# A wait for the end of each 256-token sum of squares on TensorE, in a four-layer model on one core

## The reference

```python
def rms_norm(x, g):
    xf = x.astype(jnp.float32)
    y = xf * lax.rsqrt(jnp.mean(xf * xf, axis=-1, keepdims=True) + RMS_EPS)
    return (y * g.astype(jnp.float32)).astype(x.dtype)

h = h + swiglu(rms_norm(h, norm_ffn[layer]), ffn_w_gu[layer], ffn_w_down[layer])
```

## Time and profile before

| | |
|---|---|
| three runs | 3108.95, 3109.23, 3134.92 us |
| median | 3109.23 us |
| profiled execution: span from first to last instruction | 3133.1 us |
| the profiled execution's own time (the only one of the three that holds its span) | 3134.92 us |
| TensorE products, and the time they are busy | 25968, 3121.2 us (100%) |
| VectorE, ScalarE busy | 59%, 51% |
| DMA | 551 MB, mean 176 GB/s |

### The profile page before, as it was taken

One profiled execution on the slowest core, in us unless ns is written; L12 is line 12 of the kernel. 1 busy time (PEld: TensorE's weight loads), 2 busy tenths in 40 slices (PEclk: granted clock), 3 DMA queues, 4 the chain that ended last, 5 costly groups with the idle time before them and its releaser, 6 DMA issues.

```text
span 3133.1 us, 60484 instructions
## 1 busy us (share of the span) xinstructions
PE 3121.2 (100%) x25968; PEld 3092.2 (99%) x25968; DVE 1858.3 (59%) x2028; ACT 1604.8 (51%) x2085; POOL 0.2 (0%) x4
## 2 busy tenths in 40 slices
PE   9999999999999999999999999999999999999999
PEld 9999999999999999999999999999999999999999
DVE  7655555445555477765554455547667666766664
ACT  7654433333433366754443344446657655656663
POOL 0000000000000000000000000000000000000000
PEclk9999999999999999999999999999999999999999
DMA  7335555655556555565566555655656556656554
GB/s 238 116 122 175 174 174 175 202 159 166 176 176 195 160 177 180 165 205 187 183 204 186 165 188 187 207 182 165 173 166 178 169 166 193 181 167 177 169 162 148
DMA packets 530944, 551.10 MB, mean 176 GB/s; under 512 B 15472, under 2 KB 524528, under 8 KB 529648
## 3 DMA queue, kind: packets, MB, share of 16 engines
q1 hardware_dynamic: 530800, 549.00, 56.2%
HBM read 541.56 MB, written 2.10 MB: 174 GB/s over the span
## 4 chain that ended last, share of the span: by engine, by line
PE 96%; ACT 1%; DVE 1%; DMA 0%; issue 0%; SPq 0%; ACTq 0%; DVEq 0%
PE ps L661 88%; PE ps L731 2%; PE ps L1088 1%; PE ps L1000 1%; PE ps L799 1%; PE ps L991 1%; PE ps L1008 0%; PE ps L967 0%; PE ps L907 0%; PE ps L804 0%; PE ps L830 0%; DMA raw<-mla_w_in_dram 0%; ACT w_hi L1116 0%; PE ps L963 0%; PE ps L840 0%
## 5 line engine op out<-in xcount | busy, mean ns | idle before, releaser
L661 PE MATMUL ps<-x_hi,w_hi 128*128 128x256 f32 (+1 forms) x5840 | 1648.3, 282 | 5.3 <-DVE w_lo L1775 1.6
L661 PE MATMUL ps<-x_lo,w_hi 128*128 128x256 f32 (+1 forms) x5840 | 1650.9, 283 | 0.0
L661 PE MATMUL ps<-x_hi,w_lo 128*128 128x256 f32 (+1 forms) x5840 | 1648.0, 282 | 0.0
L661 PEld LDWEIGHTS ps<-x_hi,w_hi 128*128 128x128 f32 x5840 | 1101.2, 189 | 12.6 <-issue 4.9
L661 PEld LDWEIGHTS ps<-x_hi,w_lo 128*128 128x128 f32 x5840 | 1103.1, 189 | 0.0
L661 PEld LDWEIGHTS ps<-x_lo,w_hi 128*128 128x128 f32 x5840 | 1096.4, 188 | 0.8
L1642 DVE TENSOR_TENSOR w_lo<-raw,w_hi 128x1024 fp32r<-128x1024 f32 (+3 forms) x496 | 651.0, 1314 | 565.7 <-ACT w_hi L1123 565.1
L1123 ACT ACTIVATE w_hi<-raw 128x1024 fp32r<-128x1024 f32 (+3 forms) x496 | 559.9, 1131 | 693.7 <-PE ps L661 674.9
L1636 DVE TENSOR_TENSOR w_lo<-raw,w_hi 128x1024 fp32r<-128x1024 f32 (+2 forms) x496 | 595.2, 1201 | 484.2 <-ACT w_hi L1116 481.8
L1116 ACT ACTIVATE w_hi<-raw 128x1024 fp32r<-128x1024 f32 (+2 forms) x496 | 513.2, 1036 | 375.3 <-PE ps L661 372.9
L661 PE MATMUL ps<-hid_hi,w_lo 128*128 128x272 f32 (+1 forms) x1408 | 400.9, 285 | 0.0
(11 more groups left out here) (296 smaller groups left out, 2286.0 us busy)
## 6 DMA issues: line engine op xcount, KB each, us to landing
raw<-ffn_w_gu_dram SPq DMA_DIRECT2D x176, 1024.0 KB, 5.1
raw<-w_in_dram SPq DMA_DIRECT2D x128, 1024.0 KB, 5.5
raw<-ffn_w_down_dram SPq DMA_DIRECT2D x64, 1408.0 KB, 6.5
raw<-w_out_dram SPq DMA_DIRECT2D x32, 1024.0 KB, 5.4
raw<-lru_w_in_dram SPq DMA_DIRECT2D x24, 1024.0 KB, 5.5
raw<-mla_w_o_dram SPq DMA_DIRECT2D x16, 1024.0 KB, 5.4
raw<-lru_w_o_dram SPq DMA_DIRECT2D x16, 1024.0 KB, 5.4
raw<-lru_y_gates_dram SPq DMA_DIRECT2D x8, 1280.0 KB, 5.6
```

Source lines behind the costliest of these rows:

```text
L661: mm = pe.matmul(out, l, r, start=first and k == 0 and i == 0, stop=last and k == kn - 1 and i == 2)
```

## The change

Behind the last product of `sum_squares` TensorE waits for that product's own signal, where the norm has 256 tokens. Everything else is as before.

```diff
@@ -699,6 +699,8 @@
                 else:
                     pe.wait_ge(acc_folded, folds(nm))
                 pe.matmul(bank(b, tokens), ones[:], of[:, 0, 0:tokens], start=blocks > 2, stop=True).then_inc(ss_made, 1)
+                if tokens == SEQ:
+                    pe.wait_ge(ss_made, nm.n0 + 1)
 
             def normed(nm):
                 def at_chunk(k):
```

## The result

Measured side by side, 20 runs each, the changed kernel took 3109.84 us (median; 3109.15 to 3110.49), the kernel before 3122.33 us (3108.95 to 3138.41). The ratio is 0.9946, 95% interval 0.9925 to 0.9968. Before's median is no time that a run has: its 20 runs lie in two groups, ten at 3109.0 to 3109.7 and ten at 3134.9 to 3138.4. The changed kernel's 20 all lie in the lower group.

A forecast was written before the change was run, and what follows sets the result against it. TensorE's own product rate was taken to bound the kernel. The median run of 3109.2 us, taken as short already, plus 1.4 for four waits less 0.4 regained gave 3110.2 us, range 3107 to 3113.

The forecast's parts named there:

- What bounds the kernel, and the two paces: Only TensorE's own rate sets the time; its 256-token products run at 113.3 or 117.8 ns, turning at N_FFN1's sum.
- the signs that were named: In the second feed-forward: groups at 276 and 188 ns, and near 718 us from sum to sum in place of 746.
- The price of a wait: Behind each of four 256-token sums the next product ends 0.31 to 0.38 us later; 1.4 us taken for all.
- So I expect each drained start to give the 113.3 pace.: Streams behind the four waits run at 113.3 ns: 29.2 us less in the profiled execution, 28.4 of it behind N_FFN1.
- The profiled execution would go to 3107.1.: The run of 3134.9 us loses 29.2 by the shorter pace and pays 1.4 for the waits.
- I conclude that in the two short runs the pace didn't turn at N_FFN1.: The two runs 25.8 us shorter were taken to have the second feed-forward at 113.3 ns already, which explains 28.4.
- From three runs to the median: The median run, 3109.2 us, was taken as short already: plus 1.4 for waits, less 0.4 regained, 3110.2 us.
- within 1%: The whole change was to lie inside the measurable 1%, 31 us: chance of "same" 0.94, faster 0.03, slower 0.03.
- Rival 1: Short runs also have the 118 ns stretch in the second feed-forward; the wait turns it in all: 3081.4 us, chance 0.13.
- Rival 2: The drained start behind N_FFN1's sum settles at 118 ns: 25.8 us plus the waits, 3136.4 us, chance 0.09.
- Rival 3: The waits don't act on the pace, which stays chance: 3110.6 us, or 3136 in about a quarter of cases; chance 0.06.
- Rival 4: The waits open something larger, such as a late load or other paces in the second block: over 1%, chance 0.02.

The follow-up runs named there:

- E6: Changed kernel plus a second drain, in the recurrent layer's output projection: 2 of 12 runs under 3113 us, ratio to before 1.0019; repeated, 0 of 10, 1.0036.
- E10: Kernel before plus one wait for slot_done ahead of the second feed-forward's second turn: 3 of 12 under 3113 us, median 3137.6, ratio 1.0034.
- E11: Kernel before plus one wait for slot_done at the third slot of the second feed-forward's second half: ten of ten at 3122.7 to 3124.5 us, ratio 1.0018.
- E7: Kernel before with a drain ahead of N_FFN1's sum and none behind it: 2 of 10 runs under 3113 us, ratio 1.0004.
- the first repeat: Later batch with the unaltered changed kernel beside the kernel before: 5 of 12 under 3113 us against 9 of 35, median 3135.1, ratio 0.9994.
- E1: Changed kernel with its waits set to the previous sum's signal, already given, so nothing drains: 1 of 10 under 3113 us, ratio to before 0.9992.
- E2: Changed kernel with the wait behind N_FFN1's sum only: 4 of 4 under 3113 us, ratio to before 0.9914; repeated, 4 of 9.
- E4: Changed kernel with the wait behind all nine sums, 272-token ones too: 4 of 4 at 3108.1 to 3111.8 us, ratio to before 0.9918.

## Why the prediction was right or wrong

- **What bounds the kernel, and the two paces.** Right. TensorE stays at 100% and the difference of the two profiled executions is in the main the pace of one stretch, 117.8 to 113.3 ns, with the signs that were named (276 and 188 ns, 718 us from sum to sum).
- **The price of a wait.** Right: 0.33 us against 0.31 to 0.38, 1.3 us for four against 1.4. The wake-up was 0.06 us, between its bounds.
- **"So I expect each drained start to give the 113.3 pace."** Wrong, and this is the first failed step. It rested on three starts of one execution. One of these very starts, at 1328 us, was followed by 117.8 ns in the changed kernel's trace; the table has 6 of 22 the other way behind a sum, and E6, E10 and E11 show drains that turn a short stream long. What holds is weaker: the wait takes away the sure turn to 118 (20 of 20 without it) and gives odds that vary from batch to batch.
- **The profiled execution would go to 3107.1.** The changed kernel's own took 3109.9. The term that was missed is the stretch ahead of the sum, 2.9 us, by that same start at 1328 us.
- **"I conclude that in the two short runs the pace didn't turn at N_FFN1."** Right in kind: E7, E10 and E11 have traces of a sum without a wait behind it and 113 ns behind it, each from a stream at 118. That also explains the 25.8 us where 28.4 were reckoned: a short run has the 118 pace ahead of the sum, 28.4 - 2.9 = 25.5.
- **From three runs to the median.** Wrong, the second failed step. The forecast took before's median for a short run and so the change for a mere cost of 1 us. In 20 runs ten were long, and the wait made all of its own short: a ratio of 0.9946, a gain beyond its interval, though the time itself (3109.84 against 3110.2) and "within 1%" came out. Three runs of a kernel with two groups don't give its share. That the time came out is in part luck: in the first repeat the same kernel's median was 3135.1, outside 3107 to 3113.
- **Rival 1** (the short runs have the long stretch too, 3081) is out: no run of any kernel came under 3106. **Rival 2** (the drained start settles at 118) is true in part of the runs, 7 of 12 in the first repeat, at 3134.9 to 3136.1, where it was put at 3136.4. **Rival 3** (no effect on the pace) is out by the first comparison, 20 of 20 short against 10 of 20, and by E1 against E2 and E4, 1 of 10 against 8 of 8; in the first repeat alone it would stand. **Rival 4** (something over 1%) didn't come.
- **One spacing for a width?** The Trainium skill, "TensorE: Matmul & The Clock Gate", Back-to-back issue gap, says that in a stream of weight loads and products both set the spacing, and gives one sustained figure for a width, about 81 ns at 128 columns and 131 at 512, none for 256. The traces here have several for one width at one clock: 256-token products at 113.3, 117.8, 118.7 and 120.1 ns.

In all, the changed kernel has 37 of 44 short runs over three batches; the kernel before, in the same batches, 40 of 90. The gain is 0.5% in one batch and 0.3% at the edge of its interval in another, and nothing that can be told in the third. No experiment here beat the changed kernel for sure. Left open: what sets the pace of a drained start (behind a sum the first product's 388 ns in place of 384 to 386 marks it, and doesn't explain it), why the odds differ between batches (before had 21 of 35 and 4 of 12 short in two batches on one chip, so the chip alone may not be it), why a second drain (E6, 2 of 22 short over two batches) spoils the odds of a wait 74 us later, and whether another start of the packed input than 32, 48 and 64 floats gives 113.3 ns from any start, which wasn't tried.

## What to carry to other kernels

A TensorE that is 100% busy can still run at two rates; divide stretches by their products before looking for waits, and compare the same product in several stretches. Where runs fall into groups, take enough of them to know the shares, and repeat the comparison on another chip and at another time, before a change is called a gain: the same two kernels gave 0.9946, 0.9994 and 0.9972 here. A drain cost 0.33 us here and left the pace of the stream behind it to odds, so it can pay only ahead of a long stretch, and where the stream would otherwise mostly be slow.

## What the runs showed of the hardware that was not expected

- In these traces a stream of 128x128 by 256-token fp32r products, with the input at 48 floats, kept the pace with which it started, 113.3 or 117.8 ns, for 6336 products over slots, loops and another input (up and down products), at a clock granted in full.
- A 32-bit product in two passes, whose successor's weights are loaded under it, turned a 113.3 ns stream to 117.8 in 20 cases of 20 in the traces (and 73 of 73 by the run times); draining the array behind it avoided that in 11 of 15.
- Moving the streamed input by 64 bytes either way (48 floats to 64 or 32) made every up-product of the second feed-forward 120.1 or 118.7 ns, in one group of runs, 60 or 45 us above the short runs of before. About half of that lies in the second feed-forward (28 and 23 us), the rest behind it.
- With 272 tokens there was only one pace, 125.1 ns, in the first feed-forward of every trace, with a drain behind its sum (E4) and without.
